# The sum of squares over the features as two f32r products instead of one f32 product

## The reference

```python
def rmsnorm(x, g):
    xf = x.astype(jnp.float32)
    y = xf * lax.rsqrt(jnp.mean(xf * xf, axis=-1, keepdims=True) + EPS)
    return (y * g.astype(jnp.float32)).astype(x.dtype)

h = x
for i in range(2):
    hn = rmsnorm(h, norm1[i])
    z = hn @ w_in[i]                       # pool input, q, k, v
    ...                                    # rotary, pooling mixer, dilated attention
    h = h + jnp.concatenate([pool_out, attn_out], axis=-1) @ w_out[i]
    hn = rmsnorm(h, norm2[i])
    h = h + jnp.square(jax.nn.relu(hn @ w_up[i])) @ w_down[i]
    gate = jax.nn.sigmoid(rmsnorm(h, norm3[i]) @ w_gate[i])
    h = h + gate * (p[i] @ w_ple[i])
x = rmsnorm(h, final_norm)                 # goes into the second block
```

## Time and profile before

| | |
|---|---|
| median of 3 runs | 3168.99 us (3164.33 to 3171.9) |
| the profiled execution: its own time | 3167.66 us |
| its span, first to last instruction | 3165.9 us |
| PE busy | 3121.7 us, 99% of the span |
| PE weight loads | 2518.2 us, 80% |
| DVE busy | 2045.6 us, 65% |
| POOL busy | 1713.6 us, 54% |
| ACT busy | 977.1 us, 31% |
| mean granted TensorE clock | 0.996 of full |
| share of PE in the chain that ended last | 91%, DVE 7% |

### The profile page before, as it was taken

How to read it: one execution, slowest core, us unless ns; L and a number is a source line. 1 busy time by engine, 2 the same in 40 slices (tenths; PEclk the granted TensorE clock), 3 DMA queues, 4 the chain that set the end, 5 groups by cost and what they waited for, 6 DMA issues and landing times.

```text
span 3165.9 us, 39438 instructions
## 1 busy us (share of the span) xinstructions
PE 3121.7 (99%) x14756; PEld 2518.2 (80%) x14756; DVE 2045.6 (65%) x2749; ACT 977.1 (31%) x1847; POOL 1713.6 (54%) x1544
## 2 busy tenths in 40 slices
PE   8999999999999999999999999999999999999999
PEld 6777788888888888777788888888888776688887
DVE  6656476666665664555676666664768988798323
ACT  3222253333332421222343333332432244402112
POOL 5632355666566546522465666565445533376574
PEclk9999999999999999999999999999999999999999
DMA  5211211111112122112131111112111100011112
GB/s 155 55 40 37 81 57 54 54 52 49 56 54 67 45 94 62 40 41 86 39 57 54 54 48 53 55 54 66 46 47 47 34 27 27 21 50 47 50 54 87
DMA packets 306349, 173.73 MB, mean 55 GB/s; under 512 B 61424, under 2 KB 296944, under 8 KB 306160
## 3 DMA queue, kind: packets, MB, share of 16 engines
q1 hardware_dynamic: 287904, 162.55, 17.7%
q10 hardware_dynamic: 18256, 8.67, 0.9%
HBM read 155.13 MB, written 12.91 MB: 53 GB/s over the span
## 4 chain that ended last, share of the span: by engine, by line
PE 91%; DVE 7%; issue 1%; ACT 1%; DMA 0%; ACTq 0%; DVEq 0%; SPq 0%
PE ring L1261 17%; PE ring L1263 16%; PE ring L1262 16%; PE aux L1261 5%; PE aux L1263 5%; PE aux L1262 5%; PE ring L1523 3%; PE ring L1522 3%; PE ring L1521 3%; PE aux L1523 2%; PE aux L1522 2%; PE aux L1521 2%; DVE conv_out L2670 1%; PE aux L1341 1%; PE aux L1358 1%; PE aux L1602 1%
## 5 line engine op out<-in xcount | busy, mean ns | idle before, releaser
L1010 POOL TENSOR_TENSOR w_hi<-w_raw,ones 128x512 fp32r<-128x512 f32 (+3 forms) x408 | 449.9, 1103 | 894.2 <-PE ring L1263 712.3
L1013 POOL TENSOR_TENSOR w_lo<-w_raw,w_hi 128x512 fp32r<-128x512 f32 (+3 forms) x408 | 533.9, 1308 | 32.0
L1261 PE MATMUL ring<-Q_hi,w_hi 128*128 128x512 f32 x1312 | 519.1, 396 | 0.0
L1263 PE MATMUL ring<-Q_hi,w_lo 128*128 128x512 f32 x1312 | 511.3, 390 | 0.0
L1262 PE MATMUL ring<-Q_lo,w_hi 128*128 128x512 f32 x1312 | 510.9, 389 | 0.0
L1261 PEld LDWEIGHTS ring<-Q_hi,w_hi 128*128 128x128 f32 x1312 | 246.2, 188 | 76.3 <-issue 26.4
L1263 PEld LDWEIGHTS ring<-Q_hi,w_lo 128*128 128x128 f32 x1312 | 246.3, 188 | 52.3
L1262 PEld LDWEIGHTS ring<-Q_lo,w_hi 128*128 128x128 f32 x1312 | 246.4, 188 | 50.4 <-issue 1.0
L1261 PE MATMUL ring<-P_hi,w_hi 128*128 128x512 f32 x656 | 271.0, 413 | 3.0 <-DVE pool_u L2288 1.3
L1262 PE MATMUL ring<-P_lo,w_hi 128*128 128x512 f32 x656 | 258.2, 394 | 0.0
L1263 PE MATMUL ring<-P_hi,w_lo 128*128 128x512 f32 x656 | 258.0, 393 | 0.0
(11 more groups left out here) (400 smaller groups left out, 7043.1 us busy)
## 6 DMA issues: line engine op xcount, KB each, us to landing
w_raw<-in_w_in SPq DMA_DIRECT2D x84, 512.0 KB, 3.8
w_raw<-in_w_up SPq DMA_DIRECT2D x64, 512.0 KB, 4.0
w_raw<-in_w_down SPq DMA_DIRECT2D x64, 512.0 KB, 3.4
h_scratch<-h ACTq DMA_DIRECT2D x16, 512.0 KB, 3.7
w_raw<-in_w_gate SPq DMA_DIRECT2D x16, 512.0 KB, 4.0
hx<-h_scratch SPq DMA_DIRECT2D x12, 512.0 KB, 7.8
x_raw<-in_x SPq DMA_DIRECT2D x8, 512.0 KB, 7.7
w_raw<-in_w_out SPq DMA_DIRECT2D x16, 256.0 KB, 2.8
```

The costliest lines, as they stand in the source:

```text
L1010: g.tensor_tensor(w_hi[:, slot, ks], w_raw[:, slot, ks], one.broadcast_to([P, width, P]), ALU.mult).then_inc(w_hi_ready, 1)
L1013: g.tensor_tensor(w_lo[:, slot, ks], w_raw[:, slot, ks], w_hi[:, slot, ks].bitcast(F32), ALU.subtract).then_inc(w_ready, 1)
L1261: t.matmul(o, wh, xh, start=first, stop=False)
L1263: return t.matmul(o, wl, xh, start=False, stop=last)
```

## The change

`ones` becomes an f32r tile `ones_r`, written by a product of ones with ones on GpSimd, and `ones` is its f32 view. A statistic gets two new VectorE instructions behind its last `add_square`: a copy of the sum into the f32r tile `sum_hi`, which lies on `rstd`, and a subtraction that leaves the rest in `sum_lo`, on top of `sumsq`. TensorE waits for both (`sum_ready`) and adds two f32r products with ones in place of one f32 product. `split_sum` is called at five places of the code, for 14 statistics in all, always between the last `add_square` of a half and what followed it: behind the half-0 squares at the start, behind the half-1 squares of layer 0, and, in both layers, in `sum_and_lower`, `lower_h` and the gate loop ahead of `lower`.

```diff
@@ placement and constants
+    sum_hi = place("sum_hi", [P, S], F32R, at=at_rstd)
+    sum_lo = place("sum_lo", [P, S], F32R, at=at_sumsq)
-    ones = place("ones", [P, P])
+    ones_r = place("ones_r", [P, P], F32R)
+    ones = ones_r[:].bitcast(F32)
-        g.memset(ones[:], 1.0).then_inc(eps_made, 1)
+        g.memset(ones[:], 1.0).then_inc(ones_set, 1)
+        pool.wait_ge(ones_set, 1)
+        g.tensor_tensor(ones_r[:], ones[:], ones[:], ALU.mult).then_inc(eps_made, 1)
@@ tensor
-        def sum_features(l, hf, squares_summed, *job):
+        def sum_features(l, i, hf, *job):
+            cols = half_cols(hf)
             side_starts(l, *job)
-            pe.wait_ge(summed, squares_summed)
-            t.matmul(side, ones[:], sumsq[:, half_cols(hf)], start=True, stop=True).then_inc(side_done, 1)
+            pe.wait_ge(sum_ready, stat_no(l, i, hf) + 1)
+            t.matmul(side, ones_r[:], sum_hi[:, cols], start=True, stop=False)
+            t.matmul(side, ones_r[:], sum_lo[:, cols], start=False, stop=True).then_inc(side_done, 1)
@@ vector
+        def split_sum(l, i, hf, last):
+            cols = half_cols(hf)
+            dve.wait_ge(summed, last + 1)
+            v.tensor_copy(sum_hi[:, cols], sumsq[:, cols]).then_inc(sum_high, 1)
+            dve.wait_ge(sum_high, stat_no(l, i, hf) + 1)
+            v.tensor_tensor(sum_lo[:, cols], sumsq[:, cols], sum_hi[:, cols].bitcast(F32), ALU.subtract).then_inc(sum_ready, 1)
@@ vector, start and layer 0
             add_square(k, 0, k, k)
+        split_sum(0, 0, 0, KC - 1)
...
                         add_square(k, 1, KC + k, KC + k)
+                    split_sum(0, 0, 1, 2 * KC - 1)
@@ vector, lower_h, third norm
                 add_square(f, hf, y, no, first=(f == 0))
+                if f == KC - 1:
+                    split_sum(l, 2, hf, no)
                 lower(Q_hi, Q_lo, gains[:, l, 2], f, hf, source_no(l, HN3, f, hf))
@@ vector, sum_and_lower, second norm
                 add_square(f, hf, y_no(l, Y_HN2, f, hf), sum_no(l, Y_HN2, f, hf))
+                if f == KC - 1:
+                    split_sum(l, 1, hf, sum_no(l, Y_HN2, f, hf))
                 lower(Q_hi, Q_lo, gains[:, l, 1], f, hf, source_no(l, HN2, f, hf))
@@ vector, gate loop, first norm of the next layer
                     add_square(f, hf, y_no(l, Y_HN1, f, hf), sum_no(l, Y_HN1, f, hf))
+                    if f == KC - 1:
+                        split_sum(l + 1, 0, hf, sum_no(l, Y_HN1, f, hf))
```

More of the change, by code:

```diff
@@ L598, in two_blocks @@
     eps_made = sem("eps_made")
+    ones_set = sem("ones_set")
     w_hi_ready = sem("w_hi_ready")
@@ L648, in two_blocks @@
     summed = sem("summed")
+    sum_high = sem("sum_high")
+    sum_ready = sem("sum_ready")
     rstd_ready = sem("rstd_ready")
@@ L1409, in woven @@
                 if kind == "stat":
-                    sum_features(l, args[0], sum_no(l - 1, Y_HN1, 7, args[0]) + 1 if l else KC * (args[0] + 1), *job)
+                    sum_features(l, 0, args[0], *job)
                 elif kind == "stat2":
-                    sum_features(l, args[0], sum_no(l, Y_HN2, 7, args[0]) + 1, *job)
+                    sum_features(l, 1, args[0], *job)
                 elif kind == "stat3":
-                    sum_features(l, args[0], max(sum_no(l, Y_HN3, i, args[0]) for i in range(KC)) + 1, *job)
+                    sum_features(l, 2, args[0], *job)
                 elif kind == "turn_v":
@@ L1636, in woven2 @@
                 if kind == "stat":
-                    sum_features(DEPTH, args[0], sum_no(DEPTH - 1, Y_HN1, 7, args[0]) + 1, *job)
+                    sum_features(DEPTH, 0, args[0], *job)
                 elif kind == "turn_v2":
```

## The result

The changed kernel takes 3176.7 us (median of 10 runs, 3172.05 to 3179.32), the kernel before 3168.81 us beside it (10 runs, 3164.33 to 3171.9). The ratio is 1.0023, 95% interval [1.0015, 1.0032]: slower by 7.9 us. The forecast was 3171.9 us. The profiled execution of the changed kernel took 3179.32 us, the slowest of its ten, with a span of 3177.6 us.

A forecast was written before the change was run, and what follows sets the result against it. TensorE, busy 99%, was taken as the bound. Terms: -0.2 (start) - 12 x 0.40 + 2 x 3.4 (FFN entries) + 1.1 (second block) = +2.9 us on 3167.66, 3170.6, plus 1.3 for the median: 3171.9; 8-in-10 range 3165 to 3179.

The forecast's parts named there:

- What TensorE gains: All 14 statistics: two f32r products take 0.46 us for 0.86, 0.40 us less each, 5.6 us at most.
- The copy and the subtraction: New VectorE instructions per statistic: copy 0.4 to 0.6 us, subtraction some 0.6 us where nothing is in the way.
- FFN entry, the mechanism: FFN entry, both layers: VectorE and GpSimd take turns, lower part ends 430.2 for 426.75, TensorE waits 3.4 us more per layer.
- My condition: FFN entry, each layer: TensorE waits 3 to 3.5 us for Q_lo; under 1.5 would make the forecast wrong.
- FFN entry, the clock: FFN entry: forecast took 3.4 us per layer without a clock drop; a drop would cost 1.7 us more, deciding from about 3.6.
- the prediction's own signs of being wrong: Wait for Q_lo under 1.5 us, clock below 1 behind it, or TensorE waiting at a statistic beyond the first two.
- the rival with 0.20: FFN entry: clock drops behind TensorE's wait, 1.7 us more per layer; +6.3 in all, 3175 us; chance 0.20.
- FFN end and end of layer 0: FFN end (4 statistics) and end of layer 0 (2): split hidden, no cost; at FFN end 2 us each if uncovered.
- Entry to the second block: Two statistics there: VectorE 2.4 us later against TensorE, its two waits absorb 1.3, +1.1 us at 2513.36, range 0 to 2.
- Start: Two statistics at the start: sum -0.2 us; +2.5 if GpSimd's clearing isn't late, -2.0 if the clock stays up.
- the clock rival: FFN entry: clock drop in each layer, +6.3, 3175 us, or 3178 with the start's +2.5; chance 0.20.
- a case with a chance of 0.21: Whole kernel: slower by over 0.2% (over +6.3 us), chance 0.21; within 0.73, faster by over 0.2% 0.06.

The follow-up runs named there:

- e9: Against the kernel before: last addition writes the sum as f32r, one f32r product per statistic, rest of the sum left out; 3161.44 us, 0.9972.
- e5: Changed kernel, but GpSimd waits ahead of one w_lo per layer at the FFN entry until VectorE's last half-0 lower part is written; 3171.33 us, 1.0012.
- e10: Changed kernel with the copy into sum_hi made by ScalarE instead of VectorE, subtraction still on VectorE; 3168.12 us, 0.9995 of the kernel before.
- e2: Changed kernel with the last norm's two statistics (entry to the second block) in f32 again, without the split; 3170.09 us, 1.0010 of the kernel before.
- e6: The changed kernel run again, unaltered; 3176.99 us, 1.0024 of the kernel before.
- e3: Changed kernel with the first norm of layer 0 (two statistics at the start) in f32 again, without the split; 3174.2 us, 1.0022 of the kernel before.
- e7: Changed kernel with two lines exchanged: at the FFN entry the last lower part of a half comes before the split; 3172.69 us, 1.0013 of kernel before.
- e1: Changed kernel with the second norm's four statistics (FFN entry, both layers) in f32 again, without the split; 3166.65 us, 0.9999 of the kernel before.
- e11: Changed kernel with second and last norm (six statistics) in f32 again, the other eight as two f32r products; 3166.23 us, 0.9988 of the kernel before.
- e13: Changed kernel with the copy on ScalarE and the second norm's four statistics in f32 again; 3169.15 us, 1.0004 of the kernel before.

## Why the prediction was right or wrong

**What TensorE gains: right.** 0.45 us for each statistic in the table, for 0.40 in the sum, and e9 agrees with such a gain arriving whole.

**The copy and the subtraction: right.** 0.43 and 0.6 us (start distance) where GpSimd is idle.

**FFN entry, the mechanism: right.** The turns came instruction by instruction as written, and e5 and e10 show their cause. The wait was sized at 3.4 us and measured 2.83 and 2.8. The forecast let the copy wait 1.1 us for GpSimd and the lower part end 5.1 us behind the last addition; it ended 4.5 us behind it. My condition, a wait for Q_lo of 3 to 3.5 us, was missed by 0.2.

**FFN entry, the clock: wrong.** A clock below 1 behind the wait for Q_lo was one of the prediction's own signs of being wrong, and it came. The forecast kept the full clock, the rival with 0.20 had a drop in both layers at 1.7 us each. One drop came in each of the four profiles with both waits of 2.8 us (after, e2, e6 in layer 0, e3 in layer 1), never two. It costs about 2.8 us in the changed kernel: from 427 to 445 TensorE falls 2.0 us further behind while two statistics give back 0.8; in e6 the same sum gives 1.5. The wait from which it decides was put at 3.6 us, the only one that was looked at. The low clock comes behind shorter ones too: behind 2.8 us in four of eight cases and behind 2.0 us in one of the two layers of e7, not behind 1.4 (e10). The trace of before could have said so: a wait of 2.02 us at 2704.92 has a clock of 0.64 in 2705 to 2709 behind it, and waits of 1.89 us at 1429.89 and 1.91 us at 2728.15 have the full clock. Over both layers: forecast 6.8 - 4 x 0.40 = +5.2; the table has 4.9 + 2.0 = +6.9 in the changed kernel, 3.5 + 2.0 = +5.5 in e6, and the timed e1 with its FFN entry restored is 7.6 us faster.

**FFN end and end of layer 0: right.** No wait there, only the gains of 0.45 us.

**Entry to the second block: the term that was mis-sized.** +1.1 was forecast, with 0 to 2 as its bounds; it is +4.5 between 2480 and 2512 in both profiles of the changed kernel, 0.0 in e2 and e11, and the timed e2 says 4.1 net of two statistics' gains. Two steps of mine failed. The lag of VectorE was put at 2.4 us, less 1.3 us for its own two waits. What the split itself did is less than that: the copy at 2371.63 met GpSimd and took 1.63 us, but the lower parts behind it no longer did, and at the reciprocal (2375.23 for 2368.37, with TensorE 5.45 us later) the lag is 1.4 us, still 1.6 at the next (2388.18). The rest comes afterwards, from turns: in the 40 us up to the convolution GpSimd splits weights panel by panel, and VectorE, being late, meets these instructions in another order. The lag goes to 2.7 us at the first such meeting (2397.66 for 2389.93) and is 3.85 us at the convolution, although VectorE's two waits have been used up by then. The forecast counted only what the split adds, and no turns of the instructions behind it. The value is the same in all seven profiles with the whole split at this norm; e10 and e13, with the copy on ScalarE, show that it hangs on who goes first at that meeting. And the wait was expected at 2513, where one already stood, and not at 2494, one row of weights earlier, where the trace of before shows none. There it is 3.0 us, and 3.0 us is again followed by the low clock, 1.5 us or more. The wait at 2513 went in exchange, which returned 1.1.

**Start: sized -0.2, with -2.0 as its bound if the low clock stays away.** The profiles have -2.3. The low clock didn't stay away, it came earlier, where the next wait hid it. pool_u came 1.6 us earlier for 1.0 forecast, and the wait of 1.33 us was gone, as said. Timed alone (e3) it shows nothing.

**The rest.** +2.9 was forecast between the profiled executions; +11.7 came, and +8.8 in the second profile of the same kernel; the medians differ by 7.9. Against the forecast's terms the first profile has -2.1 at the start, +1.7 at the FFN entries, +3.4 at the second block, -0.5 from gains of 0.45 for 0.40, and what the forecast had no term for: +4.2 between 1245 and 1450, +1.0 between 2512 and the last product, 1.2 behind it. In the second profile the entries have +0.3 and the step at 1245 +2.5. The step has its waits and its low clock, as told under the table, but that the change causes them is not shown: it comes with different sizes where the code of that stretch is the same (e5 -0.2, e7 -0.2, e6 +2.5). The +1.0 and the 1.2 stay open. The clock over all runs bears out a part: the mean granted clock of the changed kernel is 0.9948 (10 runs) and 0.9946 (9), of the kernel before 0.9961 (26 runs beside e6). A difference of 0.0014 is 4.4 us of 3170, an upper bound for what low clock adds, since part of it lies under waits. The time came out in the part of the range that I had given to the clock rival, and with 0.23% just beyond the bound from which I called it slower, a case with a chance of 0.21. That it fell into the range is partly luck: the point was missed by 4.8 us, and 4.2 of the first profile's 11.7 us, 2.5 of the second's 8.8, arose between 1245 and 1450, where no rival of the forecast had a price.

## What to carry to other kernels

On a kernel bound by TensorE at 99%, a gain of 0.4 us for each use is smaller than one instruction's turn on a shared port: count what the change puts between a producer and its waiting consumer, not the busy time it adds, and give that instruction to an engine that doesn't share the port (e10), or leave it out (e9), before moving it about. When a lag of an engine is traced to the next large wait, look also at the places before it where the other engine is only just not waiting. And price the low clock behind a new wait as a chance taken from rows with waits of about its length: here waits from 1.9 to 2.8 us had it in some places and executions and not in others, none from 1.3 to 1.5 us had it, and behind the first 40 us of the 14 profiles none of 3.0 us or more was without.

## What the runs showed that I had not expected

- A TensorE wait of 2.0 us (e7, layer 0) was followed by the lower clock (0.59 of full in the next 4 us), one of 1.41 us (e10) was not. The same wait of 2.8 us was followed by it in one layer and not in the other, in four profiles, and e7 has the wait of 2.0 us in both layers and the low clock in one, so the length of the wait alone doesn't decide.
- VectorE's lag at the convolution is one of two values, 3.85 us or 0.0 to 0.4 us, in thirteen profiles with leads of TensorE from -10.3 to +5.0 us; nothing lies between. With GpSimd's turns a delay of one engine comes in whole instructions, and at one meeting 0.05 us apart the order fell out differently in two kernels with the same code there (e10, e13).
- VectorE's copy from f32 to f32r, 128x512 and SBUF to SBUF, takes 0.43 us; ScalarE's takes 0.63 us, but 0.77 us pass on VectorE until it may go on.
